# Query head norms as row scales of the softmax, in a two-part hybrid network on one Trainium2 core

## What is computed

```python
def attn_heads(q, k, v, qn_g, kn_g, tabs):
    q = rms_norm(q.reshape(b_, t_, ATT_HEADS, ATT_HD), qn_g)
    k = rms_norm(k.reshape(b_, t_, ATT_KV_HEADS, ATT_HD), kn_g)
    if tabs is not None:                  # latent tokens only
        q, k = rope_2d(q, tabs), rope_2d(k, tabs)
    ...
def gqa_attend(q, k, v):
    s = jnp.einsum('bqkgd,bskd->bkgqs', q, k) * (ATT_HD ** -0.5)
    p = jax.nn.softmax(s, axis=-1)
    return jnp.einsum('bkgqs,bskd->bqkgd', p, v)

def hybrid_layer(...):
    px = split_cols(hx @ w_in + b_in)
    ya_x = conv_module(...)
    yb_x, yb_c = gla_branch(...)          # gated linear attention, 4 heads
    yc_x, yc_c = attn_branch(...)         # o * silu(gate), then @ w_attn_out
    xs = xs + gate_x * ((sigmoid(p13)*ya + sigmoid(p14)*yb + sigmoid(p15)*yc) @ w_out)
```

## Time and profile before

| | |
|---|---|
| Median of 3 runs (lowest to highest) | 3406.58 us (3406.16 to 3412.31) |
| The profiled execution's own time | 3406.26 us |
| Its span in the profile | 3404.4 us |
| PE busy, share of the span | 95% |
| DVE, ACT, POOL busy | 36%, 24%, 43% |
| Chain of work that ended last, by engine | PE 86%, DVE 6%, POOL 3%, ACT 2% |
| Mean granted TensorE clock | 0.973 |

### The profile page before, as it was taken

The page is one execution under the profiler, slowest core; times in us unless marked ns, Lnnn a source line. Parts: engine busy times, 40 slices in busy tenths (PEclk is TensorE's granted clock), DMA queues, the critical chain, the costliest instruction groups (busy, mean ns, idle before and its releaser), DMA issues.

```text
span 3404.4 us, 38854 instructions
## 1 busy us (share of the span) xinstructions
PE 3222.1 (95%) x14619; PEld 2201.7 (65%) x14619; DVE 1219.6 (36%) x2338; ACT 829.8 (24%) x1451; POOL 1447.2 (43%) x1387
## 2 busy tenths in 40 slices
PE   7999988999999999998999999999999999999988
PEld 4666655665665555466544458888994488889944
DVE  3022325543433412316544343434332233443321
ACT  4123235421111122325311112322110122322110
POOL 1788995000000069950000028776550187775600
PEclk9999998999999999999999999999999999999999
DMA  6111100023322121110156422222222222222211
GB/s 220 45 38 31 38 25 13 13 68 93 105 87 81 40 62 47 46 41 14 50 164 189 142 64 75 63 75 72 65 75 62 64 62 75 65 72 75 69 51 43
DMA packets 259322, 236.49 MB, mean 69 GB/s; under 512 B 20886, under 2 KB 257346, under 8 KB 259140
## 3 DMA queue, kind: packets, MB, share of 16 engines
q1 hardware_dynamic: 259140, 234.02, 22.7%
HBM read 231.91 MB, written 2.10 MB: 69 GB/s over the span
## 4 chain that ended last, share of the span: by engine, by line
PE 86%; DVE 6%; POOL 3%; ACT 2%; issue 2%; SPq 1%; DMA 0%; DVEq 0%; ACTq 0%; POOLq 0%
PE ps L431 38%; PE ps L1010 22%; PE ps L461 11%; PE ps L1054 2%; DVE arena L1549 2%; ACT arena L1147 2%; PE ps L711 2%; PE ps L447 1%; PE ps L1098 1%; DVE small L1758 1%; POOL arena L2092 1%; PE ps L1090 1%; PE ps L599 1%; PE ps L742 1%; DVE arena L1553 1%
## 5 line engine op out<-in xcount | busy, mean ns | idle before, releaser
L431 PE MATMUL ps<-hT,wring 128*128 128x512 f32 (+1 forms) x1568 | 577.0, 528 | 1.2 <-ACT arena L1147 1.2
L431 PE MATMUL ps<-arena,wring 128*128 128x512 f32 (+1 forms) x1280 | 489.8, 543 | 10.3 <-DVE arena L1549 10.2
L2129 POOL TENSOR_TENSOR arena<-wring 128x512 f32<-128x512 f32 x72 | 92.6, 1287 | 915.2 <-DMA wring<-in_w_in 612.6
L431 PEld LDWEIGHTS ps<-hT,wring 128*128 128x128 f32 x1568 | 302.4, 195 | 256.7 <-issue 240.8
L2092 POOL TENSOR_TENSOR arena<-arena,posi 128x512 f32<-128x512 f32 (+1 forms) x360 | 409.9, 1139 | 30.0
L461 PE MATMUL ps<-hT,wring 128*128 128x512 f32 (+1 forms) x1088 | 402.6, 525 | 1.3 <-ACT arena L1147 1.1
L431 PEld LDWEIGHTS ps<-arena,wring 128*128 128x128 f32 x1280 | 242.7, 191 | 245.8 <-issue 227.0
L1147 ACT ACTIVATE arena<-ps 128x256 f32<-128x256 f32 (+4 forms) x415 | 186.1, 449 | 709.7 <-PE ps L431 305.3
L461 PEld LDWEIGHTS ps<-hT,wring 128*128 128x128 f32 x1088 | 205.5, 193 | 168.9 <-issue 160.0
L1147 ACT ACT_TABLE_LOAD x152 | 195.0, 1283 | 373.4 <-DVE small L1978 84.9
L1549 DVE TENSOR_TENSOR arena<-arena 128x768 f32<-128x768 f32 (+7 forms) x120 | 158.9, 1324 | 324.4 <-ACT arena L1147 321.1
(11 more groups left out here) (206 smaller groups left out, 4113.5 us busy)
## 6 DMA issues: line engine op xcount, KB each, us to landing
wring<-in_w_in SPq DMA_DIRECT2D x128, 1024.0 KB, 5.3
wring<-in_w_mod SPq DMA_DIRECT2D x24, 1024.0 KB, 8.5
wring<-in_w_out SPq DMA_DIRECT2D x24, 1024.0 KB, 5.6
wring<-in_w_ada SPq DMA_DIRECT2D x24, 1024.0 KB, 5.2
wring<-in_w_conv_out SPq DMA_DIRECT2D x8, 512.0 KB, 6.1
wring<-in_w_gla_out SPq DMA_DIRECT2D x8, 512.0 KB, 4.9
wring<-in_w_attn_out SPq DMA_DIRECT2D x8, 512.0 KB, 5.9
arena<-in_x SPq DMA_DIRECT2D x1, 2048.0 KB, 8.2
```

The source lines that it names most:

```text
L431: last = eng.matmul(o_(out), a, b_, start=(i == 0), stop=(i == len(parts) - 1))
L2129: pool.link(eng.tensor_tensor(t1, w[:, 0:4, P:2 * P], w[:, 0:4, 0:P], ALU.subtract))
```

## The change

Keys are treated as before, but together: both key tiles are squared on ACT ahead of the output norm, their sums go into one bank (4), and one root and one reciprocal (`kcol`) serve both.

Queries are no longer normed. The rotation acts on the raw queries. The feature weight, times 1/8, goes into a scaled copy of the permutation (`gperm`) for the turned part and into a scalar_tensor_tensor with the cosine for the other part; context queries, which are not rotated, get a tensor_scalar with it. All four tiles' sums of squares go into one bank (7), with one root and one reciprocal into `qscale`. In attention, a query's inverse norm is one number for a row of scores: the maximum is multiplied by it on DVE (a new 128x1 tensor_tensor behind each of the 80 maxima), and the exponential takes it as its `scale` operand.

The gate tiles now stand between these steps in another pattern, the output norm's spreading comes later, and the "V" ring has four banks there (2, 3, 5, 6) where it had two. The core of the diff:

```diff
+        kcol = sb("kcol", [P, 2, 6, 2])
+        head_cols = sb("head_cols", [P, NCH * 16])
+        qscale = head_cols[:, 0:48].rearrange("p (a b c) -> p a b c", b=6, c=2)
+        gperm = pt[:, 3, TX:TX + P]
+        k_squares, q_squares = [pt[:, 2, :], last_tile], [pr[:, 0, :], pr[:, 1, :], pt[:, 2, :], last_tile]
...
+        HEAD_RINGS = {"A": [0, 1], "V": [2, 3, 5, 6]}
...
@@ PE @@
                 between = by_job("ag", C_AG, 0)
-                gla_out_norm(l, 1, between)
...
+                next(between, None)
+                gla_square_sums(l, 1)
+                rings[0] = HEAD_RINGS
...
+                head_sums("k", 4, (0, 1))
+                next(between, None)
+                key_norms(0)
+                key_norms(1)
+                turned("q", 0)
+                next(between, None)
+                turned("k", 0)
+                turned("k", 1)
+                head_sums("q", 7, range(4))
+                turned("q", 1)
+                next(between, None)
+                gla_spread(l, 1)
+                turned("q", 2)
+                next(between, None)
+                turned("q", 3)
...
-                            eng.wait_ge(*at(("hss inv", l, name, j)))
-                            job("V", ("hbc", l, name, j, sg), mms2)
@@ ACT @@
+                if p:
+                    for j in range(2):
+                        fn(k_squares[j], ak[:, j, :], ACT.Square, ("hsq", l, "k", j))
...
+                    evac(("kss", l), kcol.rearrange("p a b c -> p (a b) c"), 0, 24, ACT.Sqrt, bias=eps[:, :])
...
-                    fn(dst, src, ACT.Exp, ("probs", i, e), bias=small[:, 40 + z:41 + z], accum_out=small[:, 44 + z:45 + z])
+                    fn(dst, src, ACT.Exp, ("probs", i, e), scale=r, bias=small[:, 40 + z:41 + z], accum_out=small[:, 44 + z:45 + z])
...
+                for j in range(4):
+                    src, dst = res[:, 8 + j, u0 * P:T], q_squares[j][:, u0 * P:T]
+                    fn(dst, src, ACT.Square, ("hsq", l, "q", j))
+                next(between, None)
...
+                fn(qscale.rearrange("p a b c -> p a (b c)")[:, :, 2 * u0:12], src, ACT.Sqrt, ("free", ("qss", l)), bias=eps[:, :])
@@ DVE @@
-                            dve.link(eng.tensor_reduce(small[:, 40 + z:41 + z], src, ax, ALU.max, negate=True), ("nmax", i, e))
+                            nmax = small[:, 40 + z:41 + z]
+                            sg, hp, qb = pairs[n]
+                            dve.link(eng.tensor_reduce(nmax, src, ax, ALU.max, negate=True))
+                            tt(nmax, nmax, qscale[:, hp, UNITS[sg][qb], e:e + 1], M_, ("nmax", i, e))
...
+                ts(gperm, const[:, K_PERM:K_PERM + P], gain, None, M_, None, ("q perm", l))
+                gla_inverse(l, 1)
...
+                    stt(src[:, TC:T], src[:, TC:T], gain, rope[:, 0, :], M_, M_)
+                    tt(src[:, TC:T], src[:, TC:T], tmp[:, 0:TX], A_, ("q ready", l, j, "x"))
+                    if "c" in segs(l):
+                        ts(src[:, 0:TC], src[:, 0:TC], gain, None, M_, None, ("q ready", l, j, "c"))
+
+                rotated("q", 0)
+                rotated("k", 0)
+                rotated("k", 1)
+                rotated("q", 1)
+                gla_scaled(l, 1)
+                m.mark(("branch", l, 1), *m.at[("gla out done", l, 1)])
+                rotated("q", 2)
+                rotated("q", 3)
...
+                rcp(qscale[:, :, u0:6, :], qscale[:, :, u0:6, :], ("q inverse", l))
                 attend(l)
```

More of the change, by code:

```diff
@@ new lines, in _, with head_sums @@
+                next(between, None)
+                gla_square_sums(l, 1)
+                rings[0] = HEAD_RINGS
+                def head_sums(name, b, tiles_):
+                    pe.stage("attn_proj")
+                    key = (name + "ss", l)
+                    claim(b)
+                    eng.wait_ge(*at(("gla out read", l, 1)))
+                    for j in tiles_:
+                        eng.wait_ge(*at(("hsq", l, name, j)))
+                        for u in units(0 if name == "k" else l):
+                            src = (k_squares if name == "k" else q_squares)[j]
+                            last = eng.matmul(bank[b][:, 12 * j + 2 * u:12 * j + 2 * u + 2], src[:, u * P:(u + 1) * P],
+                                              const[:, K_HALF:K_HALF + P:64], start=True, stop=True)
+                    last.then_inc(*pe.tell(("full", key)))
+                    bank_of[key], last_on[b] = bank[b], key
@@ new lines, in turned @@
+                def turned(name, j):
+                    pe.stage("attn_proj")
+                    if name == "k":
+                        src, perm = ak[:, j, TC:T], const[:, K_PERM:K_PERM + P]
+                        eng.wait_ge(*at(("normed", l, j)))
+                    else:
+                        src, perm = res[:, 8 + j, TC:T], gperm
+                        eng.wait_ge(*at(("q perm", l)))
+                        eng.wait_ge(*at(("free", ("aq", l, j, segs(l)[-1]))))
+                    job("V", ("rot", l, name, j), lambda o_: eng.matmul(o_[:, 0:TX], perm, src, start=True, stop=True))
@@ new lines, in _ @@
+                gain = small[:, 20 + l:21 + l]
+                ts(gain, col(l, QN), 0.125, None, M_, None)
+                eng.wait_ge(*at(("gla core", (l, 1, 1))))
+                ts(gperm, const[:, K_PERM:K_PERM + P], gain, None, M_, None, ("q perm", l))
+                gla_inverse(l, 1)
+                dve.stage("rope")
+                eng.wait_ge(*at(("free", ("kss", l))))
+                rcp(kcol[:, :, :, :], kcol[:, :, :, :], ("k inverse", l))
+                for j in range(2):
+                    for sg in ("x", "c"):
+                        s0, n = SEG[sg]
+                        k = ("hbc", l, j, sg)
+                        eng.wait_ge(*at(("full", k)))
+                        stt(ak[:, j, s0:s0 + n], bank_of[k][:, 0:n], col(l, KN), ak[:, j, s0:s0 + n], M_, M_, ("free", k))
+                    m.mark(("normed", l, j), *m.at[("free", k)])
```

132 lines of the change are left out of this document (49 added, 83 removed).

## The result

The changed kernel took 3392.35 us (median of 6 runs, 3381.95 to 3395.2), the kernel before beside it 3406.37 (3405.17 to 3412.31): ratio 0.9948, 95% interval 0.9932 to 0.9963. It is faster by 14.0 us where 37.5 were forecast. The profiled execution took 3383.2 us (span 3381.3), one of the two shortest of the six (the other four took 3392.25 to 3395.2), so in the two profiles 23.1 us are gone. Two more measurements of the same kernel gave 0.9927 [0.9914, 0.9939] and 0.9932 [0.9910, 0.9954], which is 24.6 and 21.2 us.

The account below looks back on a forecast made before the run. PE was taken to bound the kernel, in attention in step with DVE. Gains of 53.8 us less 6.2, 5.5 and 4.6 for multiplications made 37.5; 3406.3 - 37.5 = 3368.8, rounded to 3369, range 3361 to 3384.

Parts of the forecast that it names:

- the section on the head stage: Head stages: PE's new list runs without waiting for ACT or DVE; 33 us gained in layer 0, 21 in layer 1.
- Its reading of the waits: Layer 0's head stage: PE, idle 17.57 us, waits at each head tile for ACT's Silu, table load and squaring.
- Rivals A: Head stages: a hand-off moves instead of going, half the idle time stays, 13.5 us less gained: 3382; chance 0.13.
- E: Head stages: PE's idle time only shadows something fixed, such as late weights, so nothing is gained: 3406; chance 0.02.
- I sum PE's new list of layer 0 from undisturbed durations: Layer 0's head stage: PE's remaining work, at durations without waits, sums to 63.0 us against 97.14 before.
- The multiplications: Attention: 80 new DVE multiplications of maxima cost 6.2 us in layer 1, 5.5 in layer 0, 4.6 more beside POOL.
- Rival D: Attention: multiplications between maximum and exponential make it slower, 99 us added if each costs 1.204 + 0.03: 3451; chance 0.01.
- rival C: Attention: the multiplications hide because PE and ACT, not DVE, release the scores: 3352.5; chance 0.06.
- The starts of attention: First scores to first maximum: layer 0 gains 2.8 us (1.7 for 4.52); layer 1 loses 1.8, plus 1.2 for clock.
- The exponential's second operand: Attention's exponentials on ACT: a second column operand adds 0.09 us each, hidden in ACT's idle time, priced at nothing.
- rival B: Attention: the exponential decides, so its longer form's 7.3 us count: 3376; chance 0.09.
- The forecast's own upper bound of 3376: Whole kernel: about 3376 us if layer 0's multiplications beside POOL cost twice the mean.

Follow-up runs that it names:

- the last experiment: The changed kernel measured a third time with no edit, beside the kernel before: 3390.5 us, ratio 0.9932 [0.9910, 0.9954].

## Why the prediction was wrong in size

*The direction, and the removal of waits,* were right. PE waits for ACT at no sum of squares, as the section on the head stage had it. Its reading of the waits was narrower than the trace: before, four of the six sums of squares waited for ACT, 10.3 of layer 0's 17.57 us, and the other 7.2 were waits for DVE; both kinds are gone. Rivals A (a hand-off moves) and E (nothing reaches the path) did not occur.

*The step that failed* is "I sum PE's new list of layer 0 from undisturbed durations", with what was built on it, that the stage would show a clock close to 1.00. A duration at full clock was taken to hold wherever PE has no gap. All but 0.83 of the 17.57 + 9.38 us of gaps went, and the clock stayed at 0.90 and 0.93: packing the sums of squares of four query tiles behind one another, and those of the keys behind the output norm's, made runs of 48 matmul records of one or two columns (40 and 32 in layer 1), and the gate tile behind each is slow. With more columns the stages came out as summed, the clock at 1.00. Of the 14.4 us that the profiles miss of the forecast, 6.35 + 2.55 = 8.9 are this; with the 50.6 that layer 1's head stage took in five other profiles it would be 1.7 more. How long such a run may be is not shown: 24 records left the next tile at 3.56 before, and at 5.41 with the sums apart, where PE had also waited 1.12.

*The multiplications* are the second step that failed, by what it left out. Their undisturbed price (0.16 each, 0.38 a pair in layer 1) was right: 5.7 at full clock for the 6.2 forecast. For layer 0, 5.5 and 4.6 for POOL were forecast as waits, 10.1; PE's idle time grew by 9.05. Beside POOL the dear ones were dearer than the mean of the earlier trace rows (25 of them averaged 0.41, up to 1.12), and still the idle time grew by a little less than the sum. What the step lacked was again the clock, which it put at nothing here though the prediction charged 1.2 for it where PE waits at the start of layer 1. It is 6.2 us of PE's work in layer 0, where the multiplications and the longer waits that they bring take it from 0.97 to 0.92. This repeats: with two multiplications a pair on DVE, PE was busy for 99.9 to 102.7 us in layer 0's attention in six profiles of six, and for 94.0 to 95.2 in the three without them on DVE. In layer 1 the two kinds overlap (76.9 to 80.2 and 76.8 to 80.1), so no such part is shown there. Layer 0's attention has 5.9 of the missing 14.4 and layer 1's 0.5. Rival D's mechanism is this one, with a price, all told (15.99 + 6.67) / 80 = 0.28 us each, far below its turning point of 0.67; rival C is refuted by the kernel without multiplications.

*The starts of attention* were right: 1.63 for 1.7, and 5.45 for 5.0 with 1.2 for the clock, which came out 0.8 too dear together.

*The exponential's second operand* costs 0.09, as the earlier trace rows said, and is hidden, shown by taking it out; rival B did not occur.

*The profile against the runs.* The sum was made against one execution. The two profiles differ by 23.1 us; the medians of the first measurement by 14.0. The last experiment shows variation of this size in stretches that no edit touches, which one profile does not show; that it makes up these 9.1 us is likely and not shown. The forecast's own upper bound of 3376, from multiplications beside POOL at twice the mean, is 3379 by its own terms; neither reaches what was measured.

## What to carry to other kernels

Take the clock of a stretch as a result of what PE executes, not only of how long it waits: here runs of matmuls with one or two columns cost PE time twice, once themselves and once in the full-size work behind them (6.68 us for 3.56). A small instruction added between two engines that run in step was paid on the path and, in layer 0, in the clock. Try it on an engine that waits in the same loop, even if it is dearer there (ScalarE's 0.29 for VectorE's 0.16 gained 13 us here). And profile a kernel more than once before you explain a difference of a few us: stretches that nothing touched differed by up to 8.5 us here.

## What was not expected of the hardware

PE was busy without a gap from 443 to 450 us and was granted 0.57 of its clock. The same sums with 128 columns took less time than with two (5.52 for 6.41 us for 48), and the gate tile behind them 3.62 for 6.68. A 128x1 multiplication on DVE with two SBUF inputs took 0.16 us while POOL was idle and up to 1.12 beside POOL's convolution, whereas the same operation on ACT took between 0.294 and 0.297 in all 80 places, those beside POOL's convolution too. And layer 0's attention, in which PE waits 0.4 us longer a pair, lost over half as much again (6.2 on top of 9.05 us) to the clock.
